# Layer norms taken by halves of 272 tokens, with the product before and the product after in halves too

## What is computed

```python
xp = _layer_norm(ALPHA * xp + yp, ln1_g[l], ln1_b[l])      # after the mixer
...
xp = _layer_norm(ALPHA * xp + fp, ln2_g[l], ln2_b[l])      # after the ConvFFN

def _layer_norm(x, g, b):
    mu = jnp.mean(xf, axis=-1, keepdims=True)
    var = jnp.mean(jnp.square(xf - mu), axis=-1, keepdims=True)
    y = (xf - mu) * lax.rsqrt(var + LN_EPS)
    return y * g + b
```

## Time and profile before

| | |
|---|---|
| median of 3 runs | 1897.36 us (1895.62 to 1899.03) |
| profiled execution | 1897.47 us |
| its span, first to last instruction | 1895.7 us |
| instructions | 35052 |
| mean granted TensorE clock | 0.974 of full speed |
| TensorE busy, matmuls | 94% |
| VectorE, ScalarE, GpSimd busy | 47%, 28%, 8% |

### The profile page before, as it was taken

The page is one execution under the profiler, slowest core; times in us unless marked ns, Lnnn a source line. Parts: engine busy times, 40 slices in busy tenths (PEclk is TensorE's granted clock), DMA queues, the critical chain, the costliest instruction groups (busy, mean ns, idle before and its releaser), DMA issues.

```text
span 1895.7 us, 35052 instructions
## 1 busy us (share of the span) xinstructions
PE 1778.9 (94%) x13474; PEld 1591.3 (84%) x13474; DVE 893.0 (47%) x1435; ACT 529.2 (28%) x742; POOL 151.3 (8%) x137
## 2 busy tenths in 40 slices
PE   8998996979999999979989989989987999999996
PEld 8765674869999999969679759849947999999995
DVE  3444355566542555352362263263256655245543
ACT  3324233242221222142222222222223322122213
POOL 0000002001000000014003013013010100000000
PEclk9999998899999999999989999999998999999998
DMA  8889784112222223212242333333323223222221
GB/s 285 297 297 302 234 306 161 45 45 89 88 99 79 78 89 105 80 38 94 104 156 97 118 133 100 129 127 105 140 89 100 71 89 106 82 78 89 89 93 47
DMA packets 84221, 234.65 MB, mean 124 GB/s; under 512 B 9777, under 2 KB 10066, under 8 KB 83778
## 3 DMA queue, kind: packets, MB, share of 16 engines
q1 hardware_dynamic: 80834, 218.97, 34.0%
q0 software_dynamic: 3328, 14.92, 2.2%
HBM read 210.05 MB, written 23.80 MB: 123 GB/s over the span
## 4 chain that ended last, share of the span: by engine, by line
PE 66%; issue 25%; DVE 5%; ACT 2%; POOL 1%; DMA 1%; SPq 0%; DVEq 0%; ACTq 0%; POOLq 0%
PE banks L1267 50%; PE banks L1612 2%; PE banks L1619 2%; PE banks L1604 1%; PE banks L1532 1%; PE banks L1294 1%; PE banks L1369 1%; PE banks L1382 1%; PE banks L1592 1%; PE banks L1330 1%; POOL y L417 1%; PE banks L1358 1%; PE banks L1635 1%; DVE x_lo L1034 1%; PE banks L1372 1%
## 5 line engine op out<-in xcount | busy, mean ns | idle before, releaser
L1267 PE MATMUL banks<-x_hi,w_hi 128*128 128x272 f32 x2624 | 551.7, 292 | 33.4 <-DVE x_lo L1034 22.3
L1267 PE MATMUL banks<-x_hi,w_lo 128*128 128x272 f32 x2624 | 545.8, 290 | 0.0
L1267 PE MATMUL banks<-x_lo,w_hi 128*128 128x272 f32 x2624 | 544.9, 289 | 0.0
L694 DVE TENSOR_TENSOR w_lo<-w_raw,w_hi 128x1024 fp32r<-128x1024 f32 (+2 forms) x228 | 284.9, 1250 | 514.6 <-ACT w_hi L462 514.5
L462 ACT ACTIVATE w_hi<-w_raw 128x1024 fp32r<-128x1024 f32 (+2 forms) x228 | 238.2, 1045 | 942.3 <-PE banks L1267 913.2
L1267 PEld LDWEIGHTS banks<-x_hi,w_hi 128*128 128x128 f32 x2624 | 415.0, 190 | 51.8 <-issue 32.5
L1267 PEld LDWEIGHTS banks<-x_lo,w_hi 128*128 128x128 f32 x2624 | 416.0, 190 | 0.0
L1267 PEld LDWEIGHTS banks<-x_hi,w_lo 128*128 128x128 f32 x2624 | 413.6, 190 | 0.0
L1267 PE MATMUL banks<-act_lo,w_hi 128*128 128x272 f32 x704 | 145.3, 287 | 0.0
L1267 PE MATMUL banks<-act_hi,w_hi 128*128 128x272 f32 x704 | 145.1, 287 | 0.0
L1267 PE MATMUL banks<-act_hi,w_lo 128*128 128x272 f32 x704 | 145.1, 287 | 0.0
(11 more groups left out here) (232 smaller groups left out, 1714.3 us busy)
## 6 DMA issues: line engine op xcount, KB each, us to landing
w_raw<-in_w_up SPq DMA_DIRECT2D x88, 512.0 KB, 3.2
kv<-in_kc SPq DMA_DIRECT2D x128, 256.0 KB, 4.8
kv<-in_vc SPq DMA_DIRECT2D x128, 256.0 KB, 4.4
w_raw<-in_w_rin SPq DMA_DIRECT2D x48, 512.0 KB, 3.3
w_raw<-in_w_dn SPq DMA_DIRECT2D x32, 704.0 KB, 4.1
s<-in_s SPq DMA_DIRECT2D x32, 512.0 KB, 7.3
out_ret_s<-s SPq DMA_DIRECT2D x32, 512.0 KB, 2.6
w_raw<-in_w_in_ab POOLq DMA_DIRECT2D x16, 512.0 KB, 6.1
```

Source lines behind the costliest of these rows:

```text
L694: V.tensor_tensor(w_lo[:, j, 0:k * P], w_raw[:, j, 0:k * P], w_hi[:, j, 0:k * P].bitcast(F32), ALU.subtract).then_inc(lo_ready, 1)
L1267: last = mm(B[:, 2 * j + half, 0:HN], a[:, j, w], x[:, kt, half * HN:(half + 1) * HN], start=kt == 0 and n == 0, stop=kt == k - 1 and n == 2)
```

## The change

A norm is taken in two halves of 272 tokens (`cols(0)`, `cols(1)`), and the halves are staggered.

- **The last pair of tiles** before a norm (`last_pair`) is multiplied half by half: both tiles for half 0, then both for half 1. While half 1 is multiplied, TensorE takes the mean of half 0 after the fourth k step of the first tile, and one row of squares of half 0 after each of the last eight k steps of the second tile. With only four k steps (norm 2) both come after the pair.
- **The mean** is taken from three f32 products, s1 and the last two rows of y, in place of one. The last two tiles are no longer added to s1.
- **The first pair of tiles** behind a norm (`first_pair`) is multiplied half by half too: k steps 0 to 5 of half 0 with the mean of half 1 after the second, then the eight rows of squares of half 1 with four steps of the second tile between them, the remaining steps of half 0, then half 1 with the second tile two k steps behind the first.
- **VectorE and ScalarE** do all work of a norm in rows of 272. Their order is written out: the splits and low halves of the next two weight tiles now stand inside the norm, as do the eight subtractions of half 1. `sq` has four slots of half a row in place of two whole ones.
- **Retention.** The four heads are written out one after the other on every engine. VectorE's wait for the scaled residual moves from ahead of the heads to ahead of each head's output sum, and its wait for GpSimd's clearing to ahead of its use.
- **The store** of the result goes out in 16 parts of half a row in place of eight.

```diff
-            for m in range(KD):
-                sp.wait_ge(y_final, m + 1)
-                sp.dma_start(A["yT"][:, m, :], y[:, m, :]).then_inc(y_stored, 16)
-
-            sp.wait_ge(y_stored, KD * 16)
+            for half in range(2):
+                for m in range(KD):
+                    sp.wait_ge(y_final, half * KD + m + 1)
+                    sp.dma_start(A["yT"][:, m, cols(half)], y[:, m, cols(half)]).then_inc(y_stored, 16)
...
             def scale_residual(n):
-                pool.wait_ge(ln_done, n * KD + KD)
+                for half in range(2):
+                    pool.wait_ge(ln_done[half], n * KD + KD)
...
+            def splits_but_two(base, n, k):
+                with act.Fori(0, n // 2 - 1) as i:
+                    for j in range(2):
+                        split(i * 2 + (base + 2 + j), j, k)
+
+            def norm(n, u):
+
                 nc.scalar.preload_act_table_set("natural_log_exp_and_others")
-                for m in range(KD):
-                    act.wait_ge(c_ready, n * KD + m + 1)
-                    if m >= 2:
-                        act.wait_ge(sq_used, n * KD + m - 1)
-                    nc.scalar.activation(sq[:, m % 2, :], y[:, m, :], ACT.Square).then_inc(sq_ready, 1)
-
-                act.wait_ge(sq_used, n * KD + KD)
-                step.add(nc.scalar.activation(halves(std[:, :]), B[:, 6:8, 0:HN], ACT.Ln, bias=eps))
-                step.wait()
-                nc.scalar.activation(std[:, :], std[:, :], ACT.Exp, scale=-0.5).then_inc(std_ready, 1)
-                for m in range(KD):
-                    act.wait_ge(scaled, n * KD + m + 1)
-                    shift = lnp[:, n, 1, m:m + 1]
-                    if n < 3:
-                        nc.scalar.activation(x_hi[:, m, :], y[:, m, :], ACT.Identity, bias=shift)\
-                            .then_inc(lnhi_ready, 1)
-                    else:
-                        nc.scalar.activation(y[:, m, :], y[:, m, :], ACT.Identity, bias=shift).then_inc(y_final, 1)
-
-            def ffn(l, k_last):
+
+                def squares(half, first, end):
+                    for m in range(first, end):
+                        q = n * 2 * KD + half * KD + m
+                        act.wait_ge(c_ready, q + 1)
+                        if half or m >= 4:
+                            act.wait_ge(sq_used, q - 3)
+                        nc.scalar.activation(sq_slot(m), y[:, m, cols(half)], ACT.Square).then_inc(sq_ready, 1)
+
+                def deviation(half):
+                    act.wait_ge(sq_used, (2 * n + half + 1) * KD)
+                    step.add(nc.scalar.activation(std[:, cols(half)], B[:, 6 + half, 0:HN], ACT.Ln, bias=eps))
+                    step.wait()
+                    nc.scalar.activation(std[:, cols(half)], std[:, cols(half)], ACT.Exp, scale=-0.5)\
+                        .then_inc(std_ready, 1)
+
+                def shift(half, first, end):
+                    for m in range(first, end):
+                        act.wait_ge(scaled, (2 * n + half) * KD + m + 1)
+                        dst, done = (x_hi, lnhi_ready) if n < 3 else (y, y_final)
+                        nc.scalar.activation(dst[:, m, cols(half)], y[:, m, cols(half)], ACT.Identity,
+                                             bias=lnp[:, n, 1, m:m + 1]).then_inc(done, 1)
+
+                squares(0, 0, 4)
+                if u is not None:
+                    split(u, 0, KD)
+                squares(0, 4, KD)
+                deviation(0)
+                shift(0, 0, 2)
+                if u is not None:
+                    split(u + 1, 1, KD)
+                shift(0, 2, 6)
+                squares(1, 0, KD)
+                shift(0, 6, KD)
+                deviation(1)
+                shift(1, 0, KD)
+
...
-            splits(U_OUT_AB, N_OUT, KD, KD)
-            norm(0)
-            ffn(0, KD)
-            norm(1)
+                        splits_but_two(base + N_UP, N_OUT, KF)
+
+            splits_but_two(U_OUT_AB, N_OUT, KD)
+            norm(0, U_FFN[0])
...
-            with act.Fori(0, H_C) as h, step.loop(h, H_C, 0):
+            for h in range(H_C):
...
+            def norm(n, base, u):
+
+                def take(half, j):
+                    i = N_OUT - 2 + j
+                    if half == 0:
+                        dve.wait_ge(half_done, 2 * n + j + 1)
+                    else:
+                        dve.wait_ge(tile_done, base + i + 1)
+                    last = V.tensor_tensor(y[:, i, cols(half)], y[:, i, cols(half)], B[:, 2 * j + half, 0:HN], ALU.add)
+                    if half:
+                        last.then_inc(evicted[j], 1)
+                    elif j:
+                        last.then_inc(s_sum, 1)
+                    else:
+                        step.add(last)
+
+                def centre(half):
+                    dve.wait_ge(m_done, 2 * n + half + 1)
+                    for m in range(KD):
+                        V.tensor_tensor(y[:, m, cols(half)], y[:, m, cols(half)], B[:, 4 + half, 0:HN], ALU.subtract)\
+                            .then_inc(c_ready, 1)
+
+                def inverse(half):
+                    own, first, var = s1[:, cols(half)], std[:, cols(half)], B[:, 6 + half, 0:HN]
+                    dve.wait_ge(std_ready, 2 * n + half + 1)
+                    step.add(V.tensor_tensor(own, first, first, ALU.mult))
+                    step.wait()
+                    step.add(V.scalar_tensor_tensor(own, var, eps, own, ALU.add, ALU.mult))
+                    step.wait()
+                    step.add(V.scalar_tensor_tensor(first, own, 3.0, first, ALU.subtract, ALU.mult))
+                    step.wait()
+                    dve.wait_ge(c_ready, (2 * n + half + 1) * KD)
+
+                def scale(half, m):
+                    V.scalar_tensor_tensor(y[:, m, cols(half)], y[:, m, cols(half)], lnp[:, n, 0, m:m + 1],
+                                           std[:, cols(half)], ALU.mult, ALU.mult).then_inc(scaled, 1)
+
+                def rest(half, m):
+                    if n < 3:
+                        dve.wait_ge(scaled, (2 * n + half) * KD + m + 1)
+                        dve.wait_ge(lnhi_ready, (2 * n + half) * KD + m + 1)
+                        V.scalar_tensor_tensor(x_lo[:, m, cols(half)], y[:, m, cols(half)], lnp[:, n, 1, m:m + 1],
+                                               x_hi[:, m, cols(half)].bitcast(F32), ALU.add, ALU.subtract)\
+                            .then_inc(ln_done[half], 1)
+
+                def tail(half, first):
+                    for m in range(first, KD):
+                        scale(half, m)
+                        rest(half, m - 1)
+                    rest(half, KD - 1)
+
                 step.wait()
-                step.add(V.scalar_tensor_tensor(halves(s1[:, :]), B[:, 6:8, 0:HN], eps, halves(s1[:, :]),
-                                                ALU.add, ALU.mult))
-                step.wait()
-                step.add(V.scalar_tensor_tensor(std[:, :], s1[:, :], 3.0, std[:, :], ALU.subtract, ALU.mult))
-                step.wait()
-                dve.wait_ge(c_ready, (n + 1) * KD)
-                scale(0)
-                for m in range(KD):
-                    if m < KD - 1:
-                        scale(m + 1)
-                    if n < 3:
-                        dve.wait_ge(scaled, n * KD + m + 1)
-                        dve.wait_ge(lnhi_ready, n * KD + m + 1)
-                        V.scalar_tensor_tensor(x_lo[:, m, :], y[:, m, :], lnp[:, n, 1, m:m + 1],
-                                               x_hi[:, m, :].bitcast(F32), ALU.add, ALU.subtract)\
-                            .then_inc(ln_done, 1)
-
-            def ffn(l, k_last):
+                take(0, 0)
+                take(0, 1)
+                dve.wait_ge(s_sum, 2 * n + 1)
+                centre(0)
+                take(1, 0)
+                inverse(0)
+                scale(0, 0)
+                scale(0, 1)
+                if u is not None:
+                    low(u, 0, KD)
+                take(1, 1)
+                dve.wait_ge(evicted[0], (base + N_OUT) // 2 + 1)
+                dve.wait_ge(evicted[1], (base + N_OUT) // 2 + 1)
+                dve.sem_inc(s_sum, 1)
+                rest(0, 0)
+                scale(0, 2)
+                rest(0, 1)
+                scale(0, 3)
+                rest(0, 2)
+                if u is not None:
+                    low(u + 1, 1, KD)
+                scale(0, 4)
+                rest(0, 3)
+                scale(0, 5)
+                rest(0, 4)
+                centre(1)
+                tail(0, 6)
+                inverse(1)
+                scale(1, 0)
+                tail(1, 1)
+
...
-            dve.wait_ge(y_scaled, 1 + 2 * KD)
-            dve.wait_ge(zeroed, 3)
+            ffn(0)
+            norm(1, U_RET - N_OUT, U_RET)
...
+                dve.wait_ge(y_scaled, 1 + 2 * KD)
...
+            def half_step(j, half, k, hi, lo, kt):
+                w = slice(kt * P, (kt + 1) * P)
```

(88 more changed lines are left out.)

126 lines of the change are left out of this document (54 added, 72 removed).

## The result

The changed kernel takes 1918.83 us (median of 5 runs, 1912.76 to 1920.23), the kernel before 1898.83 in the runs beside it. The ratio is 1.0095, interval 1.0080 to 1.0111: 18 us slower by the ratio, 20 by the medians. The prediction was 1915 us, slower.

The account below looks back on a forecast made before the run. TensorE, busy for 94% of the span, was taken as the bound, so only its standstills or needless work could be won. Norms 0 to 3 at +5.6, +4.1, +7.6 and +0.2 summed to +17.5, giving 1915 us; range 1902 to 1924.

Parts of the forecast that it names:

- (a), (d): TensorE's last pair and first pair: f32 halves 0.455 us each, plus breaks of 1.0 and waits of 0.9 us.
- (b), (c): After T, the last pair's end: first half step at T + 5.8, sixth k step of half 0 at T + 13.9.
- (e): Ahead of half 1: chain of 4.5 us, 1.5 covered, third wait about 3 us; first step at T + 25.2.
- rival 4: Halved VectorE instructions cost half: 2.5 us a norm less, 1907 us; chance 0.10 including a like shortfall.
- (g): Clock falls to 1.2 GHz in the first wait, 1.8 us; possible second fall 0 to 2 us, taken as 0.9.
- Rival 3: Clock stays low through the squares of half 1: 5 us more at three norms, 1925 to 1930 us; chance 0.13.
- (h): Behind the first pair at norms 0, 1 and 2: third tile's split and low half leave 1.5 us open.
- (i): Norm 1: moving VectorE's wait for GpSimd's residual removes a 1.7 us stall; rotary steps some 4 us later, covered.
- (j): Norm 2, behind tiles of only 4 k steps: 0.7 us of low half exposed, 7.8 us in place of 6.0.
- (k): Norm 3, from the end of the matmuls' own time to the last shift: 25.8 us against 25.6, +0.2.
- (l): Four heads written out: costs nothing, up to 3 us if new code is fetched late.
- Rival 1: The overlap holds: TensorE never waits again after its first half step, loss 19.5 us a norm, 1891 us; chance 0.07.

Follow-up runs that it names:

- e8: Changed kernel with each row of squares of half 0 multiplied twice at norms 0, 1 and 3; 1930.68 us, ratio 1.0173 to the kernel before.
- e3: Changed kernel with the low half of the next product's first weight tile moved ahead of the first half's inverse deviation; 1915.58 us, ratio 1.0088.
- e4: Changed kernel with half 0 finished ahead of the centring of half 1, ScalarE and TensorE reordered to follow; 1914.63 us, ratio 1.0076.
- e11: Changed kernel with unused f32 products in TensorE's three waits at norms 0 to 2, the first 11 ahead of the weights wait; 1912.75 us, ratio 1.0085.
- e2: Changed kernel with GpSimd's scaling of the residual after norm 1 moved behind the rotation of head 0; 1912.41 us, ratio 1.0081.
- e6: e1 with VectorE's two waits for GpSimd moved as in the change, whole rows everywhere; 1891.88 us, ratio 0.9964 to the kernel before.
- e1: Kernel before, with only its loop over the four heads written out on every engine; 1895.97 us, ratio 0.9984.
- e12: e5 with 8 unused f32 products ahead of TensorE's first wait and 7 in the later one; 1898.09 us, ratio 1.0002 to the kernel before.
- e5: Changed kernel with the edits of e2, e3 and e4 together; 1903.1 us, ratio 1.0025 to the kernel before.

## Why the prediction was right, and where its terms were not

Time and sign were right, 1915 against 1918.83; the sum of 17.5 stands against 18 by the ratio, 20 by the medians and 21.0 by the trace. The mechanism forecast for the norms, three waits in each, came as written. That the total came so near is in part luck: in the profiled execution the first three norms cost 24 us, of which the collision at norm 1 and most of the low clock were not in the sum, and the heads and the part ahead of norm 0 gave 3.5 back.

- **(a), (d) f32 work and breaks.** Norm 0 as a whole cost 4.7 us at the third tile, forecast 5.6. The f32 halves cost 0.455 each, as e8 shows. The 1.9 us for breaks at changes of kind don't exist: this part was mis-sized, and the third wait's end came at T + 24.3 in place of T + 25.2.
- **(b), (c) the two waits.** T + 5.9 and T + 13.9, forecast 5.8 and 13.9. e3 shows that the low half stands in the first, e4 that the centrings stand in the second.
- **(e) the third wait.** 2.73, forecast about 3. But e4 shows that the way to it has more than one layer: with VectorE's queue out of the way TensorE's own work, at the low clock in part, is as late.
- **VectorE's pace.** Eight subtractions take 2.86 us, 0.35 apart, and scale and `x_lo` come 0.41 apart. The rule of the Trainium skill, "VectorE: DVE Perf Modes", section "The TRN2 errata", fits the duration of one (0.44), and read as a pace it would have made 1924; the starts decided, so rival 4 and that sum both fell.
- **(g) the clock.** The first fall costs nothing that can be seen at norm 0, the later ones more than 0.9: 1.4 us behind the third wait at norms 0 and 2 (e11), and 2.1 and 1.6 in the full tiles behind norms 1 and 2, which I had not. Rival 3 named the right thing: the squares of half 1 ran at full clock at norm 0, but their first part at the low one at norm 2 (1480 to 1482), and the stretch took 1.8 us more there.
- **(h) the wait on `w_lo`.** 1.82 and 1.87 us, forecast 1.5; the 0.3 are GpSimd again, the low half takes 1.68 there.
- **(i) norm 1: the step that failed.** "GpSimd's scaling then delays the first rotary steps by some 4 us, with over 30 us of products covering that." It delayed VectorE. The wait removed had kept the low half out of GpSimd's way; without it the low half took 5.00 us and TensorE waited 5.20. e2 and e6 show this from both sides. The earlier trace rows had the stall of 1.7, and I took it for a pure loss. Norm 1 cost 6.25 us at the third tile and 2.1 behind it, forecast 4.1.
- **(j)** 0.75 for 0.7 of the first low half. Norm 2 as a whole was +9.35 at the third tile for 7.6, and +11.0 at the low half for the fifth tile (1451.62 to 1510.88, before 1441.94 to 1490.24). In e2, whose code for norm 2 is the same, the latter stretch is 55.54 us (1446.63 to 1502.17) in place of 59.26. So 3.7 of it are falls of the clock that another execution doesn't have.

```profile
1453.83 0.39 PE L1339 MATMUL banks<-m_hi,w_hi 128*128 128x272 f32 x1 [0.75 <-DVE w_lo L726]
```

- **(k)** +0.35 for +0.2, the second take's wait 3.87. The agreement is luck to some 2 us, by the two rows of squares at norm 3 above.
- **(l) the heads written out.** Forecast 0 to +3. e1 as a whole is some 3 us faster, though its trace doesn't show them in the heads, and the heads of the changed kernel are 3.0 shorter for a reason that stayed open. That hid most of what the collision cost.

Rival 1, the overlap, asked for a second and third wait under 1 us in sum; they were 5.0 at norm 0. e12 is the nearest to it that repairs reach, and it is no faster than before.

What was shown: the collision (e2, e6), the price of f32 work (e8), the low half in the first wait (e3), that writing the heads out costs nothing (e1). Shown by the trace alone, not beyond the intervals of the runs: the clock's share in the changed kernel. Between e5 and e12 the ratios differ by 0.0023, with intervals that just touch.

## What to carry to other kernels

As far as this kernel shows, staggering two halves pays only where an engine's queue holds enough work of the other half at each point of the chain. Here two half chains run through the same in-order queues of VectorE, ScalarE and TensorE, so each half waits behind the other's, and the f32 work added to TensorE is paid in full. A wait that looks like a loss may be what keeps two engines apart: before removing it, look at what would then run side by side. And when a product is cut so that its tiles end together, whatever the second tile covered lies open.

## What the runs showed of the hardware

- **VectorE and GpSimd block each other, and not evenly.** A low half (two tensors read) beside GpSimd's scalings (0.71 us each) took 5.00 us in the changed kernel and 5.29 in e6. In both it ended 1.1 us after the last scaling, about its own length alone (1.22), while the scalings lost nothing (5.58 and 5.57 us for eight). At norm 0 the low half took 1.68 and one scaling 1.69 us. The Trainium skill, "SBUF — State Buffer", section "SBUF: two separate sides", says that the two share one pair of ports, held by whoever starts first for one instruction. That fits norm 0. At norm 1 VectorE waited through some six instructions in a row, which the page's "for the whole instruction" does not say; what decides between the two cases stayed open.
- **A change of kind costs nothing.** f32 products put between fp32r half steps add 0.455 us each and no more.
- **Work for nothing keeps the clock up.** With products of constants in the waits the granted clock was 1.00 where it had been 0.50 to 0.63, and at norms 0 and 2 the work behind the third wait took 9.15 and 9.13 in place of 10.54 us. In whole rows the same won nothing.
- **Unrolling a loop over four heads** on five engines was not slower but 0.16% faster (0.04 to 0.27); the trace doesn't show where.
